# TensorE's exit from the experts' rounds, ScalarE's closing order, and four reorderings in a two-layer encoder step

## The reference

```python
q, k, v, u = split_projection(h, w_in[l])
a = diff_attention(q, k, v, ...)                # 4 heads, two softmax maps each
p = pool_mixer(u, ...)
h = layer_norm(ALPHA * h + concat(a, p) @ w_out[l], ln1_g[l], ln1_b[l])       # LN1
# routing: softmax over 16 experts, the best of 4 groups, then the top 2 in it
probs = softmax(h @ router_w)
y = sum over e of combine[:, e] * (silu(h @ w_gate[e]) * (h @ w_up[e])) @ w_down[e]
h = layer_norm(ALPHA * h + y, ln2_g[l], ln2_b[l])                             # LN2
```

## Time and profile before

| | us |
|---|---|
| median of 3 runs | 983.27 (983.20 to 985.94) |
| profiled execution | 983.06 |
| its span on the core | 981.3 |
| PE busy in the span | 943.9 (96%) |
| DVE busy | 822.3 (84%) |
| ACT busy | 657.7 (67%) |
| POOL busy | 260.4 (27%) |
| mean granted clock of TensorE | 0.985 |

### The profile page before, as it was taken

One profiled execution on the slowest core, in us unless ns is written; L12 is line 12 of the kernel. 1 busy time (PEld: TensorE's weight loads), 2 busy tenths in 40 slices (PEclk: granted clock), 3 DMA queues, 4 the chain that ended last, 5 costly groups with the idle time before them and its releaser, 6 DMA issues. The chain is left out here.

```text
span 981.3 us, 15260 instructions
## 1 busy us (share of the span) xinstructions
PE 943.9 (96%) x5118; PEld 785.0 (80%) x5118; DVE 822.3 (84%) x1211; ACT 657.7 (67%) x941; POOL 260.4 (27%) x343
## 2 busy tenths in 40 slices
PE   4999999999999999999989999999999999999994
PEld 4998867688888888888779988787888888888883
DVE  7977667789989899899866676588999898998997
ACT  4446541378888888888745566317788888888882
POOL 1433343471111111110323333425211111111012
PEclk8999999999999999999989999999999999999998
DMA  9863850599999999998894033529999999999965
GB/s 353 281 174 121 266 190 38 189 366 407 379 363 367 364 366 367 374 374 323 234 298 158 27 133 136 190 82 348 411 401 373 369 367 369 367 366 375 331 196 151
DMA packets 85550, 278.28 MB, mean 284 GB/s; under 512 B 8771, under 2 KB 11067, under 8 KB 85470
## 3 DMA queue, kind: packets, MB, share of 16 engines
q1 hardware_dynamic: 66880, 240.40, 66.9%
q0 software_dynamic: 11040, 21.14, 7.5%
q10 hardware_dynamic: 7566, 15.96, 4.7%
HBM read 266.51 MB, written 30.37 MB: 303 GB/s over the span
## 5 line engine op out<-in xcount | busy, mean ns | idle before, releaser
L1565 DVE TENSOR_TENSOR w_lo<-ring,w_hi 128x1024 fp32r<-128x1024 f32 x256 | 303.1, 1235 | 36.0 <-ACT w_hi L2200 33.6
L2200 ACT ACTIVATE w_hi<-ring 128x1024 fp32r<-128x1024 f32 x256 | 261.4, 1060 | 39.6 <-PE PS L1094 26.6
L1046 PE MATMUL PS<-w_hi,x_hi 128*128 128x512 f32 x512 | 163.9, 401 | 0.0
L1051 PE MATMUL PS<-w_lo,x_hi 128*128 128x512 f32 x512 | 160.7, 395 | 0.0
L1046 PE MATMUL PS<-w_hi,x_lo 128*128 128x512 f32 x512 | 160.0, 394 | 0.0
L1572 DVE TENSOR_TENSOR w_lo<-ring,w_hi 128x1024 fp32r<-128x1024 f32 x128 | 153.6, 1220 | 4.4 <-ACT w_hi L2213 4.4
L2213 ACT ACTIVATE w_hi<-ring 128x1024 fp32r<-128x1024 f32 x128 | 135.6, 1061 | 29.6 <-PE PS L1051 27.9
L2565 POOL DMA_INDIRECT M<-xs,idx x30 | 56.2, 1874 | 235.4 <-PE PS L1025 204.0
L1046 PEld LDWEIGHTS PS<-w_hi,x_lo 128*128 128x128 f32 x512 | 96.3, 188 | 23.2
L1051 PEld LDWEIGHTS PS<-w_lo,x_hi 128*128 128x128 f32 x512 | 96.5, 188 | 22.1
L1046 PEld LDWEIGHTS PS<-w_hi,x_hi 128*128 128x128 f32 x512 | 94.0, 189 | 19.6
(11 more groups left out here) (292 smaller groups left out, 1609.7 us busy)
## 6 DMA issues: line engine op xcount, KB each, us to landing
ring<-in_w_gate SPq DMA_DIRECT2D x32, 2048.0 KB, 14.4
ring<-in_w_down SPq DMA_DIRECT2D x32, 2048.0 KB, 14.8
ring<-in_w_up SPq DMA_DIRECT2D x32, 2048.0 KB, 15.6
ring<-in_w_in SPq DMA_DIRECT2D x8, 2048.0 KB, 16.8
ring<-in_w_out SPq DMA_DIRECT2D x4, 2048.0 KB, 8.8
ys<-H SPq DMA_DIRECT2D x2, 3072.0 KB, 20.0
H<-ys POOLq DMA_DIRECT2D x12, 512.0 KB, 8.4
M<-in_cache_k ACTq DMA_DIRECT2D x8, 512.0 KB, 3.7
```

What stands on the lines that cost most here:

```text
L1046: pe.matmul(PS[:, n, :], x[:, c:c + P], w_hi[j][:, k * 512:(k + 1) * 512], start=(j == 0 and k == 0 and x is x_hi[par]), stop=False)
L1051: mm = pe.matmul(PS[:, n, :], x_hi[par][:, c:c + P], lo[:, k * 512:(k + 1) * 512], start=False, stop=(j == 3 and k == 1))
L1565: dve.tensor_tensor(lo, w, w_hi[j][:, :].bitcast(F32), ALU.subtract).then_inc(up_lo, 1)
L2200: act.activation(w_hi[j][:, :], quarter(3 * par + n, j)[0], ACT.Copy).then_inc(up_hi, 1)
```

## The change

The change has six parts.

1. In `moe_round` of PE the load of `more_rounds` moves from behind `end_sums` to ahead of it, behind the wait for `half_end`. In layer 0 the branch is turned round: `turn_h(l, 0)` now stands in the arm that falls through, the other rounds (with a `turn_h(l, 0)` of their own) in the `Else` behind it, and `turn_h(l, 1)` behind both. After `turn_h(l, 0)` PE jumps over the `Else`.
2. ACT's closing of layer 0: `bias_rounded` ahead of the squares of block 2; `turned_hi(0)` ahead of the squares of block 3; `diagonal(3)` behind `turned_hi(2)`.
3. `route`: `keys_turned(0)` and the last logits ahead of `first_x(1)` (only layer 0 has one there); `first_x(last - 1)` ahead of `keys_turned(2)`; `rank(last)` ahead of `keys_turned(3)`. `out_proj`: the first logits one product group earlier.
4. DVE's start: `turned_h(3)` ahead of `w_split(0, 1)`.
5. DVE's LN1 and `choose`: one conversion (L1467) less per block, one reduction no longer waits for the one ahead of it; in the last block the router's offsets ahead of the shift, and in layer 0 the shift inside `choose`. ACT issues the loads of `gb` inside the attention loop.
6. End of layer 1: DVE takes the gain of block 0 between the means of blocks 1 and 2, and the last shift in two halves of 512 columns, each with its own store on SP.

```diff
@@ SP, end
+                for half in range(2):
+                    sp.wait_ge(h_done, ln_count(LN2[-1], j) + half)
+                    sp.dma_start(dst[:, 512 * half:512 * (half + 1)], H[:, j, 512 * half:512 * (half + 1)]
+                                 ).then_inc(y_out, 16)
@@ PE, route
+                keys_turned(l, (0,))
+                logits(l, last)
                 for n in range(1, last - 1):
                     first_x(l, n)
-                keys_turned(l, (0,))
-                logits(l, last)
...
                 keys_turned(l, (1,))
+                first_x(l, last - 1)
                 keys_turned(l, (2,))
-                first_x(l, last - 1)
+                rank(l, last)
                 keys_turned(l, (3,))
-                rank(l, last)
@@ PE, moe_round and the layers' loop
                 if seated:
+                    pe.wait_ge(routed, l + 1)
+                    more = pe.value_load(more_rounds[0:1, 0:1], min_val=0, max_val=3)
                     end_sums()
+                    return more
...
-                moe_round(l, rb, 0, True)
-                pe.wait_ge(routed, l + 1)
-                more = pe.value_load(more_rounds[0:1, 0:1], min_val=0, max_val=3)
+                more = moe_round(l, rb, 0, True)
                 R = more + 1
-                with pe.If(more > 0):
-                    pe.wait_ge(sum_kept[l], len(tiles_of(l)))
-                    with pe.Fori(1, R) as r:
...
                 if l + 1 < DEPTH:
-                    turn_h(l, 0)
+                    with pe.If(more < 1):
+                        turn_h(l, 0)
+                    with pe.Else():
+                        other_rounds(l, rb, R)
+                        turn_h(l, 0)
                     turn_h(l, 1)
+                else:
+                    with pe.If(more > 0):
+                        other_rounds(l, rb, R)
@@ DVE, choose
-                then(dve.tensor_reduce(score[p], pairs6[p], X, ALU.max))
-                then(dve.tensor_reduce(best[p, 0:1], score[p], X, ALU.max))
+                did(dve.tensor_reduce(score[p], pairs6[p], X, ALU.max))
+                then(dve.tensor_reduce(best[p, 0:1], pairs6[p].rearrange("p g n -> p (g n)"), X, ALU.max))
...
-                then(dve.tensor_copy(e12[p], where8[p, 0:2]))
@@ DVE, closing of layer 1
-                    for n in range(len(tiles_of(l))):
-                        mean_taken(l, n)
+                    mean_taken(l, 0)
+                    mean_taken(l, 1)
                     gain_at = gained(l, 0)
-                    for n in range(len(tiles_of(l))):
+                    mean_taken(l, 2)
+                    for n in range(2):
                         shifted(l, n, gain_at)
-                        if n + 1 < len(tiles_of(l)):
-                            gain_at = gained(l, n + 1)
+                        gain_at = gained(l, n + 1)
+                    shifted(l, 2, gain_at, (slice(0, 512), slice(512, D)))
@@ DVE, start
+            turned_h(3)
             w_split(0, 1)
-            turned_h(3)
@@ ACT, closing of layer 0
+                bias_rounded(l)
                 squared_rows(l, 2)
                 diagonal(l, 1)
+                turned_hi(l, 0)
                 squared_rows(l, 3)
-                turned_hi(l, 0)
-                bias_rounded(l)
                 diagonal(l, 2)
-                diagonal(l, 3)
                 turned_hi(l, 1)
                 turned_hi(l, 2)
+                diagonal(l, 3)
@@ ACT, attention loop
+                    if j == 13:
+                        act.wait_ge(u_out, 128 * l + 64)
+                        act.wait_ge(v_out, 48 * (l + 1))
+                        load_gb(LN1[l], t["ln1_g"][l], t["ln1_b"][l])
```

More of the change, by code:

```diff
@@ L949, in out_proj @@
                 turn_sum(l, 0)
-                out_part(l, 1, (6, 7))
+                out_part(l, 1, (6,))
+                logits(l, 0)
+                out_part(l, 1, (7,))
                 if l == 0:
                     o_turned(l, 12)
-                logits(l, 0)
                 pe.wait_ge(xo_lo, xo_count(l, "frames1"))
@@ L1199, in moe_round, with other_rounds @@
                 if seated:
+                    pe.wait_ge(routed, l + 1)
+                    more = pe.value_load(more_rounds[0:1, 0:1], min_val=0, max_val=3)
                     end_sums()
+                    return more
+            def other_rounds(l, rb, R):
+                pe.wait_ge(sum_kept[l], len(tiles_of(l)))
+                with pe.Fori(1, R) as r:
+                    pe.wait_ge(idx_in, rb + r - l)
+                    for n in range(len(order(LN1[l]))):
+                        mm = index_part(l, n, 7, True)
+                    mm.then_inc(idx_ps, 1)
+                    moe_round(l, rb, r, False)
             pe.wait_ge(early_in, 16)
@@ L1448, in choose @@
                     made_hot(l, n - 1, placed_at)
+                if between:
+                    between()
                 dve.wait_ge(ex_done, 4 * l + n + 1)
@@ L1905, in _ @@
                         o_scale(l, 12)
-                    if n > 0 and n + 1 < len(tiles):
+                    if n + 1 < len(tiles):
                         gained_at = ln_h_gain(q, n, gained1[n % 2][0:rows])
@@ L1913, in _, with late_shift @@
                     dve.wait_ge(hx_ps, 2 * (TURNED[q] + n) + 2)
-                    ln_h_shift(q, n, gained1[n % 2][0:rows], gained_at)
-                    offset_at = offsets(l, n)
+                    def late_shift():
+                        ln_h_shift(q, n, gained1[n % 2][0:rows], gained_at)
+                    if last:
+                        offset_at = offsets(l, n)
+                        if l > 0:
+                            ln_h_shift(q, n, gained1[n % 2][0:rows], gained_at)
+                    else:
+                        ln_h_shift(q, n, gained1[n % 2][0:rows], gained_at)
+                        offset_at = offsets(l, n)
                     if not last:
                         placed_at = seat(l, n - 1) if n >= 1 else 0
-                    choose(l, n, offset_at, placed_at)
+                    choose(l, n, offset_at, placed_at, late_shift if last and l == 0 else None)
                 seat(l, len(tiles) - 1)
```

28 lines of the change are left out of this document (12 added, 16 removed).

## The result

The changed kernel took 988.77 us (median of 11 runs, 986.25 to 993.82) against 985.54 for the kernel before in the same runs: 1.0043 times as long, with a 95% interval of 1.0027 to 1.0060. A second measurement gave 1.0052 (1.0034 to 1.0069). The forecast was a gain of 0.1%, with a range that ended at 985.3. The profiled execution took 986.25 us with a span of 984.5, 3.2 more than the one before.

What follows compares the result with a forecast made beforehand. PE's gaps and tail were taken to bound the kernel. From 983.06 us, 1.0, 0.1 and 0.5 off, 0 and 0.65 on gave 982.1, and 982.3 with the runs' median 0.2 higher; range 979.7 to 985.3.

Steps and rivals of the forecast that it cites:

- What bounds the kernel: Whole kernel: PE's gaps and tail count; the longest gap, 2.68 us, is the jump over the other rounds.
- Start: Kernel start: PE's wait of 1.01 us for block 3's `FThi` goes; 1.0 us off, at least 0.7.
- Routing: Routing: 0.1 us off in layer 0, 0.5 off in layer 1; earlier logits in `out_proj` give 0.
- The load: PE's load of `more_rounds` ahead of the end sums: exposed, costing 1.5 us per layer, from 0.9 to 1.9.
- the fall of the clock over the sums: Rival at 0.11, end sums of both layers: the load's idle time lowers the clock; 985.5 us, up to 987.
- The closing: End of layer 0: jump's stall changes places with one block's transposes; projection at 510.9 against 510.97, no change.
- I take 4.9, the middle between them: Layer 0's closing: PE's new jump behind the first block delays the second by 4.9 us, between 3.9 and 5.8.
- The cheap jump: Rival at 0.20, layer 0's closing: the jump is cheap in its new place; 2.3 us off the closing, 980.0.
- The end: End of layer 1: DVE's work ends 1.1 us later, last store lands 0.45 sooner; net 0.65 us on.
- The sum: Whole kernel: 1.0, 0.1 and 0.5 off, 0 and 0.65 on, from 983.06 to 982.1; forecast 982.3 us.
- Within 0.3%: Whole kernel's measured time: no change, between 980.3 and 986.2 us; chance 0.68.
- slower: Whole kernel's measured time: above 986.2 us, from the fallen clock and the closing's far bound; chance 0.10.

Runs made afterwards that it cites:

- a_again: The changed kernel measured once more without any edit, against the kernel before: ratio 1.0052.
- a_old_pe: The changed kernel with PE's load of `more_rounds` and its branch as in the kernel before, all else changed: ratio 0.9983 to the kernel before.
- c_hold: Changed kernel with load ahead of last down products, next layer's weights held until first block's transposes, block 2's mean before block 0's gain: ratio 0.9965 to kernel before.
- a_pool_free: The changed kernel without GpSimd's deviation of layer 1's last block, DVE using block 1's instead: ratio 1.0060 to the kernel before.

## Why the prediction was wrong, point by point

- **What bounds the kernel** was read rightly. The jump, not DVE's gain, is the gap of 2.68: with a short jump it is gone.
- **Start:** 1.0 foretold. The gap of 1.01 went, and the products behind stood 0.5 to 0.7 earlier. The first product of the projection stood 0.5 later in this execution (at 19.2; between 18.6 and 19.5 in all profiles), so that 1.0 fits.
- **Routing:** 0.1 and 0.5 foretold, and 0 for the earlier logits in `out_proj`. The products laid side by side give 1.0 won at the end of layer 0's `out_proj`, 0.3 of it inside it, and 1.2 at the first expert, so 0.2 in the routing. In layer 1 `out_proj` gave 0.3 and the routing 0.6. The two routings were read well; the 0 for `out_proj` was wrong, since the same 0.3 per layer is there in other profiles with the new order (a_again, a_old_pe). In layer 0 the gaps merged into one wait of 1.42 for the mask; in layer 1 PE's first expert now waits 0.62 for ACT's copy, as the prediction said of ACT.
- **The load:** 1.5 in each layer foretold; the gap grew by 1.4 and by 1.15. The size was right (1.4 to 1.9 and 1.0 to 1.6 over the seven profiles with the exposed load). What failed beside it was the chance of 0.11 for the fall of the clock over the sums: it came in layer 0 in four of these profiles, though in layer 1 in only one, where the rival wanted both. The changed kernel's mean clock is 0.984 and 0.9825 in its two measurements, against 0.9866. By the slope above that is 1.5 to 2.3 us, a third to a half of the loss.
- **The closing:** this is the step that failed most. "I take 4.9, the middle between them" was the mean of two jumps in other traffic, one of them with GpSimd's transfers ahead of it, none with weights. 6.5 and 8.0 from dispatch to first work were measured (498.3 to 504.8, 502.0 to 510.0), because three transfers of 2 MB are issued just ahead of where the jump now stands. The trace of before had that issue at 498.9, 3.5 us behind the old jump's dispatch. The prediction moved the jump past it, with the exposed load's 1.4 us on top, without looking at what else lay there. For the two later blocks it took 2.6 and 2.0 us, and 3.4 and 2.0 came, with the clock at half over the first of them; the old second block, which it put at 504.55, stood at 504.80. The rule of the Trainium skill that was weighed there (Runtime: NRT & Kernel Launch, section "Instruction fetch mechanics") spoke for the stall, and the runs agree: 3.3 to 7.9 us where the target is far, 0.3 where it is near.
- **The cheap jump,** rival at 0.20: it exists (3.3 to 3.8 us with 2 us of it under the first block), but only ahead of the weights' issue, and in the changed kernel it never showed.
- **The end:** 0.65 foretold, 1.9 measured in the tail. What was foretold is the landing of the last store, and that was nearly right: from the last down product SyncE's drain came 0.4 later. The step that failed is to take the landing for the end. GpSimd's drain came 1.9 later and was last, which the prediction's sum has no term for.
- **The sum:** front and routing gave 2.2 (foretold 1.6) and the load cost 2.5 (3.0). The closing beyond the load and beyond a fall of the clock cost 1.0 against the undisturbed 18.7: 22.51 less 1.4 for the load and 1.4 for the clock (the two later blocks took 5.44 us, and 4.05 in c_hold at full clock) leaves 19.7. The forecast had 1.5 off there. The end beyond the load cost 0.8. Together 2.1 lost; by the spans at equal clock 3.0, and 4.2 or more with the clock. What lies between 2.1 and 3.0 is open; the jump alone differed by 1.6 us between the two profiles of this kernel. "Within 0.3%" was given 0.68, "slower" 0.10.

## What to carry to other kernels

Before a taken branch is moved, look at what the transfer queues do in the four microseconds ahead of its dispatch: its code is fetched through the same engines, and a bulk load that is issued just ahead of it took the stall here from 3.8 to as much as 7.9 us. A hold of that load by one semaphore, until the fetch is out, cost nothing here. A register load belongs where its engine still has work queued, never behind a wait for the engine's own last product. And a gap that is made on TensorE can be paid twice, once in itself and once in the clock of the work behind it: that came in five of the fourteen places where the load was exposed.

## What the runs showed of the hardware

- **GpSimd's drain at the program's end** ended 6.55 us behind its last operation in all 17 profiles. It was the last thing before the end in 16 of them; only in a_pool_free, where the last operation came early, the store's landing was. With the old order at the end the two are 0.3 apart, so the last small operation on GpSimd counts as much as the last store.
- **A far jump on TensorE** takes 3.3 to 3.8 us from dispatch where its fetch started about 1 us behind the dispatch, 3.7 to 6.5 in the old place and in layer 1, and 6.2 to 7.9 behind 2 MB transfers. Its record holds all of that, while on ACT the record of a far jump shows 38 ns, though the next instruction came 3.9 us later.
- **The profile's releaser** for the longest gap was wrong in the same way in both kernels: the gain that the block needed was over 3 us or more before PE went on. The sequencer's own rows show the branch.
- **The granted clock** differs from execution to execution of one kernel, from 0.981 to 0.991 in one set of 35 executions of the kernel before. At 0.57 us for a thousandth that is 5.7 us, more than any single edit here is worth. Verdicts on a few microseconds need many runs, or the clock beside the time.
